# Sampled attention of a hybrid decoder step: keys turned by VectorE in 32x32 blocks and multiplied in 32x32 tiles, in place of full transposes on TensorE

## The reference, cut to what matters

```python
s = jnp.einsum('bqhmd,bkhmd->bhmqk', q, k) * (HEAD_DIM ** -0.5)   # plus bias by distance
p = jax.nn.softmax(logits, axis=-1)
w = p[:, :, 0] - lam * p[:, :, 1]
o = jnp.einsum('bhqk,bkhe->bqhe', w[..., :past], v_past) + jnp.einsum('bhqk,bkhe->bqhe', w[..., past:], v)
```

## Time and profile before

| | us |
|---|---|
| median of 2 runs | 2018.13 (2017.17 to 2019.09) |
| the profiled execution | 2017.05 |
| its span, first to last instruction | 2015.2 |
| TensorE busy | 1967.5 (98%) |
| VectorE busy | 1312.9 (65%) |
| ScalarE busy | 937.4 (47%) |
| DMA, mean over the span | 91 GB/s |
| mean granted clock of TensorE | 0.997 of 2.4 GHz |

### The profile page before, as it was taken

One profiled execution on the slowest core, in us unless ns is written; L12 is line 12 of the kernel. 1 busy time (PEld: TensorE's weight loads), 2 busy tenths in 40 slices (PEclk: granted clock), 3 DMA queues, 4 the chain that ended last, 5 costly groups with the idle time before them and its releaser, 6 DMA issues. The chain is left out here.

```text
span 2015.2 us, 35806 instructions
## 1 busy us (share of the span) xinstructions
PE 1967.5 (98%) x11872; PEld 1801.8 (89%) x11872; DVE 1312.9 (65%) x2891; ACT 937.4 (47%) x1705; POOL 37.0 (2%) x126
## 2 busy tenths in 40 slices
PE   6999999999999999899999999999999999999998
PEld 6999999999999999767768798999999998989896
DVE  6767667676676767666644485666657574748476
ACT  5766665657575757555554241322223131314033
POOL 0000000000000000000020000000000000000000
PEclk9999999999999999999999999999999999999999
DMA  6411111111111112599973121111111120202012
GB/s 197 150 58 54 58 53 57 53 57 53 57 53 57 53 55 76 199 349 338 342 278 110 35 81 32 55 42 53 42 44 52 32 63 22 73 22 73 5 50 100
DMA packets 167452, 183.25 MB, mean 91 GB/s; under 512 B 11045, under 2 KB 139589, under 8 KB 167349
## 3 DMA queue, kind: packets, MB, share of 16 engines
q1 hardware_dynamic: 166137, 181.24, 27.3%
q10 hardware_dynamic: 1212, 0.81, 0.1%
HBM read 162.82 MB, written 24.46 MB: 93 GB/s over the span
## 5 line engine op out<-in xcount | busy, mean ns | idle before, releaser
L1250 PE MATMUL ps<-h_hi,w_hi 128*128 128x384 f32 (+1 forms) x1152 | 387.0, 336 | 5.1 <-DVEq L967 3.4
L1250 PE MATMUL ps<-h_hi,w_lo 128*128 128x384 f32 (+1 forms) x1152 | 376.8, 327 | 0.0
L1250 PE MATMUL ps<-h_lo,w_hi 128*128 128x384 f32 (+1 forms) x1152 | 376.8, 327 | 0.0
L2410 PE MATMUL ps<-h_hi,f_w_hi 128*128 128x320 f32 (+1 forms) x1136 | 370.7, 326 | 0.8 <-PEq L1563 0.8
L2410 PE MATMUL ps<-h_hi,f_w_lo 128*128 128x320 f32 (+1 forms) x1136 | 370.4, 326 | 0.0
L2410 PE MATMUL ps<-h_lo,f_w_hi 128*128 128x320 f32 (+1 forms) x1136 | 370.2, 326 | 0.0
L2489 ACT ACTIVATE yc<-ps,f_prm 128x384 f32<-128x384 f32 x144 | 93.5, 654 | 555.7 <-PE ps L2410 382.8
L2390 PE MATMUL ps<-d_hi,act 128*128 128x512 f32 x816 | 257.0, 390 | 0.5 <-issue 0.5
L1250 PEld LDWEIGHTS ps<-h_hi,w_hi 128*128 128x128 f32 x1152 | 217.3, 189 | 9.0 <-issue 4.0
L1250 PEld LDWEIGHTS ps<-h_lo,w_hi 128*128 128x128 f32 x1152 | 217.4, 189 | 0.6
L1250 PEld LDWEIGHTS ps<-h_hi,w_lo 128*128 128x128 f32 x1152 | 217.0, 188 | 0.0
(11 more groups left out here) (301 smaller groups left out, 3181.0 us busy)
## 6 DMA issues: line engine op xcount, KB each, us to landing
k<-in_cache_k SPq DMA_DIRECT2D x64, 512.0 KB, 5.8
v_raw<-in_cache_v SPq DMA_DIRECT2D x64, 512.0 KB, 6.2
w_raw<-in_w_in SPq DMA_DIRECT2D x48, 512.0 KB, 4.0
f_raw<-in_w_up SPq DMA_DIRECT2D x48, 512.0 KB, 3.9
f_raw<-in_w_down SPq DMA_DIRECT2D x24, 512.0 KB, 3.5
bias<-bias_tiles_dram SPq DMA_DIRECT2D x8, 576.0 KB, 3.7
merged_dram<-mg SPq DMA_DIRECT2D x8, 544.0 KB, 2.7
ow_raw<-in_w_out SPq DMA_DIRECT2D x8, 512.0 KB, 7.5
```

Source lines behind the costliest of these rows:

```text
L1250: last_ = pe.matmul(bank(s)[:, 0:n], w[:, W_SLOT[g], k, :], x[:, k, off:off + n], start=(k == 0 and i == 0), stop=(k == KT - 1 and i == 2))
L2410: l_ = pe.matmul(ps[:, e % 6, 0:n], w[:, p, k, :], x[:, k, off:off + n], start=(k == 0 and i == 0), stop=(k == KT - 1 and i == 2))
```

## The change

Of the sampled stage, the stage before and the allocation around them:
- Each page of keys, [128 positions, 1024], is turned by one VectorE instruction in 32x32 blocks, in place (`turn_keys`, 8 a sample). The head's dimension then lies in 32-row pieces, and the positions of a page in quarters i.
- The scores are f32 products of 32x32 tiles: 32 rows of keys by 32 query columns (`qd` holds, for each piece J of 32 dimensions and each row group i, the queries placed so that a column group h gets heads h and h+4), moving four pages x 32 positions = 128 columns. For two parts of four pages, two head groups e, four pieces j, four column groups h, four row groups i: 256 products a sample, accumulated into bank i, partitions 32h. The new keys have eight products of their own in bank 4. Part 0 waits for four turned pages (for sample 0, eight), part 1 for all.
- No high and low parts of keys, no copies of them, no row sums. ScalarE writes the queries of b+1 behind the exps of b, in 20 small copies. The bias-and-max reads the four banks, and again for the new keys. The rows' order, and with it the bias's and `pair_select`'s, is changed; the bias is loaded in quarters with runs of 32 elements.
- Order on TensorE in turn b: weights of b-1, fold of b-2, scores of b, values of b-1. SP: keys of b+1 behind `score_done` b, then values of b page by page behind `page_done`. The loops of the engines are written out.
- Value pages 0 to 3 of sample 0 are loaded in the last turn of `heads`, behind the last two key pages, and 4 to 7 behind the last merged store. TensorE's transposes at the end of `heads` go.
- The way out: tiles 0 and 1 of `out_tile`, halves k 0 to 3, stand behind the weights of sample 7 and the fold of sample 6, before the last values; ScalarE splits m0 and w0 to w3 before it copies the last weights; w_out rows 0 to 3, m0 and m1 are loaded before the values of sample 7.

```diff
@@ heads, sync
+            def load_values(pages):
+                for n in pages:
+                    load_page(ins["cache_v"], n, c.v_raw[:, n, :], c.v_in[n])
...
                         if last and ahead:
                             load_pages(done_last.index(s))
+                            if s[1] == GB:
+                                load_values(range(0, 4))
...
                         sp.dma_start(c.merged_dram[bass.ds(f, 1), :, :].rearrange("a p n -> p (a n)"),
                                      mg[:, :]).then_inc(mg_out, 16)
+                        if last:
+                            load_values(range(4, NPAGES))
@@ sampled_and_out, sync
+            load_constants()
+            load_keys(1)
+            for x in range(2):
+                sp.dma_start(vn_raw[NS * x:NS * (x + 1), :], v_new).then_inc(vn_in, 16)
+            for b in range(1, DEC_B):
+                if b < LAST:
+                    load_keys(b + 1)
+                else:
+                    sp.wait_ge(score_done, LAST)
+                    load_w(0)
+                    load_m(0)
+                    load_m(1)
+                load_values(b)
+            sp.wait_ge(score_done, DEC_B)
+            load_w(1)
@@ tensor
-            def turn_keys(b, u, h):
...
+            def scores(b):
+                keys = k_raw[b % 2]
+                pe.wait_ge(qd_done, b + 1)
+                for hf in range(2):
+                    pe.wait_ge(kt_done, NPAGES * (b + 1) if hf or b == 0 else NPAGES * b + 4)
+                    if b > 0 and hf == 0:
+                        pe.wait_ge(ttr_done, 2 * b)
+                    for e in range(2):
+                        for j in range(NQ):
+                            for h in range(HH):
+                                J = NQ * (HH * e + h) + j
+                                for i in range(NQ):
+                                    part = slice(32 * i, 32 * i + 32)
+                                    pe.matmul(S[32 * h:32 * h + 32, i, 128 * hf:128 * hf + 128], qd[part, J, :],
+                                              keys[part, 4 * hf:4 * hf + 4, 32 * J:32 * J + 32],
+                                              start=(e == 0 and j == 0), stop=(e == 1 and j == NQ - 1))
...
+            for b in range(DEC_B):
+                if b >= 1:
+                    turn_weights(b - 1)
+                if b >= 2:
+                    fold_heads(b - 2)
+                scores(b)
+                if b >= 1:
+                    values(b - 1, 0)
+                    values(b - 1, 1)
+            turn_weights(LAST)
+            fold_heads(LAST - 1)
+            out_tile(0, range(0, 4))
+            out_tile(1, range(0, 4))
+            values(LAST, 0)
+            values(LAST, 1)
             out_tile(0, range(4, KT))
-            fold_heads(DEC_B)
+            fold_heads(LAST)
@@ scalar
+            def queries(b):
+                if b > 0:
+                    act.wait_ge(score_done, b)
+                for j in range(NQ):
+                    src = c.q_new[32 * j:32 * j + 32, :, DEC_T * b:DEC_T * (b + 1)]\
+                        .rearrange("p (e h) t -> p e h t", e=2)
+                    for i in range(NQ):
+                        q = qd[32 * i:32 * i + 32, j, :]
...
+                        act.activation(dst, src, ACT.Copy)
...
+            for b in range(DEC_B):
+                if b >= 1:
+                    copy_weights(b - 1)
+                if b >= 2:
+                    copy_o2(b - 2)
+                exps(b)
+                if b < LAST:
+                    queries(b + 1)
+            for x in OUT_SPLITS[0:5]:
+                split_out(*x)
+            copy_weights(LAST)
+            copy_o2(LAST - 1)
@@ vector
+            def turn_keys(b, n):
+                dve.wait_ge(c.k_in[b % 2][n % 4 if b == 0 else n // 2], 32 * (b // 2 + 1))
+                keys = k_raw[b % 2][:, n, :]
+                dve.transpose(keys, keys).then_inc(kt_done, 1)
...
+            for b in range(DEC_B):
+                for n in range(NPAGES):
+                    turn_keys(b, c.k_first[n] if b == 0 else n)
+                if b >= 2:
+                    fold_rows(b - 2)
+                if b == 0:
+                    signs()
+                softmax(b)
+                weights(b)
```

More of the change, by code:

```diff
@@ L1374, in _ @@
             body(H - 1, False, True)
[L1375 to L1385, removed]
 def pair_select():
     row = np.arange(128)
-    head, m, t = row // 16, row // 8 % 2, row % 8
+    head, m, t = HH * (row // 16 % 2) + row // 32, row // 8 % 2, row % 8
     sel = (np.arange(NS)[None, :] == (head * DEC_T + t)[:, None]).astype(np.float32)
@@ L1444, in strip, with page_keys @@
         return o2[32 * q:32 * q + 32, :]
[L1446 to L1463, removed]
+    def page_keys(x):
+        return x[:, 0:PAST].rearrange("p (i k) -> p i k", i=NQ)
     def own_rows(hf):
@@ L1538, in bank_of @@
     def bank_of(t):
[L1539 to L1551, removed]
-        for b in range(6, DEC_B + 1):
-            body(b, b % 2)
-    def has(b, d):
-        return not isinstance(b, int) or 0 <= b - d < DEC_B
-    def at_start(b):
-        return isinstance(b, int) and b == 0
+        return 0 if t % 2 else 2
     with nc.Block() as block:
@@ L1678, in _, with load_keys, load_values @@
-            all_turns(sp, body)
-            sp.wait_ge(qkh_done, 8 * DEC_B)
+            def load_keys(b):
+                if b >= 2:
+                    sp.wait_ge(score_done, b - 1)
+                for n in range(NPAGES):
+                    load(b, n, ins["cache_k"], k_raw[b % 2][:, n, :], c.k_in[b % 2][n % 4 if b == 0 else n // 2])
+            def load_values(b):
+                for n in range(NPAGES):
+                    sp.wait_ge(page_done, NPAGES * (b - 1) + n + 1)
+                    load(b, n, ins["cache_v"], v_raw[:, n, :], v_in[n])
@@ new lines, in values @@
+            def values(b, run):
+                if run == 0:
+                    pe.wait_ge(ptc_done, 2 * b + 2)
+                    if b > 0:
+                        pe.wait_ge(ots_done, b)
+                for n in RUNS[run]:
+                    if n == NPAGES:
+                        pe.wait_ge(vn_in, 32)
+                    else:
+                        pe.wait_ge(v_in[n], 16 * (b + 1))
+                    for hf in range(2):
+                        cols = slice(512 * hf, 512 * (hf + 1))
+                        v = v_raw[:, n, cols] if n < NPAGES else vn_raw[:, cols]
+                        last = pe.matmul(strip(hf, n), pt_sb[:, n, 32 * hf:32 * hf + 32], v,
+                                         start=(n < 2), stop=(n in (NPAGES - 1, NPAGES)))
+                    if n < NPAGES:
+                        last.then_inc(page_done, 1)
@@ L1872, in keys @@
-            def keys(b, h):
-                for hf in range(2):
-                    act.wait_ge(tk_done, 16 * b + 2 * h + hf + 1)
-                    if hf == 0 and not (at_start(b) and h < 2):
-                        act.wait_ge(qkh_done, 8 * b + h - 1)
-                    act.activation(kt_hi[:, h % 2, 512 * hf:512 * (hf + 1)], tb[hf], ACT.Copy)\
-                       .then_inc(kthi_done, 1)
+                    dst = qn[part, :, :].rearrange("p (e h) (f k t) -> p e f k h t", e=2, f=2, k=2)
```

476 lines of the change are left out of this document (150 added, 326 removed).

## The result

The changed kernel takes **2074.39 us** (median of 2 runs, 2072.68 to 2076.1), 1.0284 times the time before (95% interval 1.0267 to 1.03). The forecast was 1986, its range 1973 to 2021. The profiled execution took 2072.68, its span is 2070.8: 55.6 more than before.

| us from the span's start | before | after |
|---|---|---|
| first bias-and-max starts | 858.6 | 870.2 |
| seven turns later, the eighth | 1030.9 | 1077.2 |
| one turn | 24.6 | 29.6 |
| first transpose of the normed rows | 1061.0 | 1116.5 |

A forecast was written before the change was run, and what follows sets the result against it. The DMA was taken to wait for a compute ring, 24.6 us a turn; with a 17.0 us chain the DMA's 20.4 would bind. First normed transpose 31.5 us earlier: 2017.05 - 31.5 = 1985.5, said 1986, range 1973 to 2021.

The forecast's parts named there:

- the DMA's floor: Sampled stage: a turn's 8.39 MB need 20.4 us at 411 GB/s, against 24.6 us a turn before.
- 1.21 a transpose: VectorE in the sampled stage: eight page transposes at 1.21 us, 9.7 us a turn; bounds 0.6 and 2.4 each.
- Rival C: VectorE's transpose takes two cycles an element, 2.4 us; a turn of 26.3, the kernel 2035; chance 0.07.
- ScalarE's 20 copies hidden: Sampled stage: 20 small query copies a turn, 0.22 us each, 4.4 us, hidden by the turning of keys.
- what matters is how many run at once: TensorE's scores: 16 products share a round if rows and columns compose, 3.5 us a turn; 4.5 taken.
- Rival B: Rows and columns don't compose, four score products at once: 14 us, a turn 23.6, the kernel 2018; chance 0.07.
- half scores 2.3 us: TensorE: half of the 4.5 us of scores wait for the last turned page, adding 2.3 to a 17.0 us turn.
- A: Rival: TensorE fed too slowly, 14 ns an instruction; scores 14.5 us, a turn 24.0, the kernel 2018; chance 0.09.
- D: Rival: 57 ns an instruction, scores 58 us, the kernel 2356; slower than before from about 15 us of scores; chance 0.11.
- The clock, costed at nothing: TensorE idle while keys are turned may run at 1.2 GHz: scores 7 us, chain 18.3, still under 20.4.
- The start: SP's four added value-page issues open the stage 4.4 us later, at 839.0; first scores end at 854.7.
- The tail: Stage's end: first transpose of the normed rows at 1029.5 in place of 1061.0, gain 31.5 us.

The follow-up runs named there:

- looped: Changed kernel with 256-column score products (half the score instructions), TensorE's program for samples 2 to 7 as three passes of a two-sample loop: 2002.43 us, 0.9926 of before.
- half_products: Changed kernel with 256-column score products and value products ahead of the next scores, second half of the heads' score products left out: 1994.63 us.
- twice: Changed kernel with 256-column score products, a sample's 128 products executed two times over in a loop: 2051.32 us.
- values_tail: Changed kernel with 256-column products, value products ahead of next scores, early splits and half of output tile 0 back ahead as before: 2026.68 us.
- one_start: Changed kernel with 256-column score products, sample 0's last four value pages issued inside the stage, behind sample 1's keys: 2020.35 us.
- looped_w_early: On looped: first four w_out rows and merged tiles 0 and 1 loaded ahead of sample 6's values, split before the last softmax: 1998.52 us.

## Why the prediction was wrong, point by point

- **The bound of the kernel before, the DMA's floor: right.** 20.4 us a turn at 411 GB/s was forecast; looped held 20.7 to 21.3 at 393 to 405, half_products 20.7 at 408.
- **VectorE: right.** 1.21 a transpose was taken, 1.207 measured. From the scores' end to the first transpose 3.9 us (forecast 4.6), the eight together 9.1 (9.7). Rival C is out.
- **ScalarE's 20 copies hidden: right.** 0.25 and 0.22 each, 4.9 us, done before the scores could start but for one wait of 0.5 us.
- **TensorE, "what matters is how many run at once": right in kind, mis-sized, and not what mattered.** 78 starts a microsecond at full clock and 53 at 1.2 GHz are 6.6 and 9.6 us for 512 MATMULs, where 4.5 was taken and 3.5 was the lower bound. By the 0.11 us of one MATMUL of 128 columns at full clock, four at once would give 36 a microsecond and sixteen 145, so some nine ran at once. Rival B (four) is out, and rows and columns compose only in part at 128 columns. This slip alone would have cost nothing: half the scores at 4.8 us make a turn of 3.9 + 9.1 + 4.8 + 0.4 = 18.2, under 20.4. The Trainium skill (TensorE: Matmul & The Clock Gate, section "Wait — 56ns, not 53.3ns?") would have 25 ns from start to start at least; 128 starts within 1.65 us, 13 ns apart, contradict it, and the measurement decides.
- **TensorE, half scores 2.3 us: the step that failed.** In the turn of sample 3 it was 16.7 us from the last transpose (937.4) to the last score product (954.1). That turn is 3.9 + 9.1 + 16.7 + 0.7 for the new keys and the hand-over = 30.4 us, against 4.6 + 9.7 + 2.3 + 0.4 = 17.0 in the forecast; of the 16.7, three waits for instructions take 10.6. I priced 1024 instructions by the pace of bursts of 4 and 16, too short to run into such a wait, and called their supply a rival (A) or a bound (D) without asking what supplies them. The page of before had the row, 43 packets of q8 with 0.1% of the DMA, and the prediction doesn't use it. The share says nothing here: each packet is 16 KB for 256 instructions, and its latency is waited for. A turn issues 1172 TensorE instructions (1024 for the scores, 148 for the rest), 4.6 packets. Some of these come while TensorE waits for turned pages; in the sample above 434 instructions ran before the first wait. Three in each sample are waited for, the 24 waits of 71.9 us. The Trainium skill (Runtime: NRT & Kernel Launch, section "Instruction fetch mechanics") states the refill by 16 KiB blocks of 256 instructions, with 2048 of them held for TensorE: a loop of some 1320 was held here and one of some 2400 was not, which agrees. That the refill is "mostly hidden", as it says there too, the 24 waits of the scores contradict.
- **Rivals.** A ("TensorE is fed too slowly") was the mechanism in kind, at 14 ns an instruction; measured were 1024 in 19.3 us, 19 ns. D's 57 ns was too much, but its line, slower from about 15 us of scores a turn, fits the 19.3. Both had worked as a pace of TensorE; the runs twice and looped show it as a price of new program text. The range ended at 2021 because A was closed off at 24 us a turn.
- **The clock, costed at nothing: right while the DMA sets the turn** (looped: 20.7 at a clock of 0.84), wrong at the stage's end in values_tail, where two half tiles took 8.6 us each in place of 5.7.
- **The start.** The opening was forecast at 839.0 and came at 840.1, here with SP's four issues as forecast:

```profile
834.50 0.36 SPq L708 DMA_DIRECT2D merged_dram<-mg  x1
835.63 3.94 SPq L632 DMA_DIRECT2D v_raw<-in_cache_v  x4
840.10 1.77 SPq L1576 DMA_DIRECT2D sbias<-sbias_dram  x2
```

  That the first four pages' bytes "only lie in front of some small row stores" missed SP's wait for those stores; with the issues gone (one_start) it took their place. The first scores took 20.3 us in place of 6, and the first bias-and-max, at 870.2, came 15.5 us behind the forecast's end of the first scores, 854.7.
- **The tail: short by 4 us.** From the last bias-and-max to the first normed transpose it is 39.4 us, 30.1 in the kernel before, where half of tile 0 (5.5 us) ran beside the last softmax and the page products of sample 6 (4.5 us) were done by then. The new order puts both behind, and the forecast's own times had that in them: eighth scores' end 854.7 + 17.0 + 6 x 20.4 = 994.1, first transpose 1029.5, 35.4 us. What it had too short are two waits, for GpSimd's low parts under the half tiles and for the copy of `o2` behind four splits; looped_w_early shortened them by 2.1 and 0.8 us and got 1.8 us back, since the page products of sample 6 took 1.1 longer. That the order makes the rest is read from the traces alone.

## What to carry to other kernels

Count a stage's instructions as well as their columns. Beyond the some 430 that were there when a stretch of scores began, each 256 new ones on TensorE came 3.5 us apart with an idle DMA and 6.2 us beside page loads, 14 and 24 ns an instruction. If small tiles are wanted, make each pass more columns (256 in place of 128 halved the score instructions and brought 55 us) and let the rest come from a loop short enough to be kept. And a wait that the profile calls "issue", in bursts of equal length, is to be laid beside the instruction queue's packets before anything is reordered.

## What the runs showed of the hardware that was not expected

- Products of 32x32 tiles on four row groups and four column groups overlap, and each still has its price beside the columns. Of 128 columns 78 f32 MATMULs start in a microsecond at 2.4 GHz and 53 at 1.2 GHz (the first two of the burst windows above). Of 256 columns it is 53 and some 33. Here first half_products, a whole burst, then looped, 5 us from a burst's start:

```profile
910.30:912.70 2.40, 2.39 (x128) 1.82 (x128) 1.00 1.03 410
...
937.08:942.08 5.00, 4.99 (x165) 3.86 (x168) 0.50 1.03 411
```

  So twice the columns cost 1.5 times the time, and half the clock costs the same as twice the columns. An estimate from these rates: some 7 ns a MATMUL with its load, and 6 ns for each 128 columns at full clock.

- Instructions compete with data for the DMA: from burst to burst 6.2 us beside page loads and 3.5 without, 3.0 and 1.6 us of it a wait. The time is lost before the packet starts (3.8 us and 1.1 in the pair of bursts above), not behind it (2.4 in both).
- A loop's second pass brought no transfer at some 1320 instructions of body, and all of them at some 2400.
- VectorE turns 128x1024 f32 in place, in 32x32 blocks, in 1.20 us, and the next starts 1.13 us behind.
